# Expert products ordered by part: both chunks' high part first, then both chunks' low part

## The chip, the cores and the metric

The kernel runs on one core of a Trainium2 chip. The metric is the device time in microseconds (us) of one execution.

## The reference, cut to what matters

Two transformer blocks are computed for 256 tokens of width 1024, in float32. The first block ends with a mixture of 32 experts, of which each token takes 4:

```python
def expert_block(args):
    rows, e = args
    xb = xt[rows]
    hb = xb @ w1[e] + b1[e]                       # w1[e]: 1024 x 2048
    g, u = hb[:, :D_EXPERT], hb[:, D_EXPERT:]
    g = jnp.minimum(g, SWIGLU_LIMIT)
    u = jnp.clip(u, -SWIGLU_LIMIT, SWIGLU_LIMIT)
    glu = g * jax.nn.sigmoid(g * SWIGLU_ALPHA)
    return ((u + 1.0) * glu) @ w2[e] + b2[e]      # w2[e]: 1024 x 1024
```

The change touches the products with `w1[e]` and `w2[e]` alone. Ahead of them lie modulation, attention branches and the router; behind them a second block with four SwiGLU feed-forward layers, one more for the context, a neighbourhood attention and a short convolution.

## The kernel before

**Parts.** Float32 accuracy comes from splitting each operand in two numbers of a rounded type (`fp32r`), a high and a low part. For an expert's weight, ScalarE copies the loaded slot into a high buffer (`high`, L895), VectorE subtracts that from the slot and writes the low part over it (`low`, L2258), and TensorE multiplies both with the tokens. The tokens' own two parts lie side by side in the 128 columns of one stationary operand (64 tokens, high and low), and the weights stream past it as the moving operand, 512 columns at a time. So one chunk of 128 rows of weights needs four matmuls: two parts by two halves of 512 columns.

**Slots.** Weights come in slots of 1 MB: two chunks of 128 rows by 1024 columns. They land in a ring of 8 places (`RING2`). There are 4 buffers for high parts (`HIGHS`). A slot's life is: the DMA, issued by SyncE as soon as the slot 8 before it has been used (L679); ScalarE's high part, as soon as the slot 4 before it has been used and the DMA has landed; VectorE's low part; TensorE's 8 matmuls (L1557), the last of which signals "used".

**Turns.** A loop of 16 turns takes two experts each, 0 and 1 of the pair, in 24 slots: 0 to 3 gate of expert 0, 4 to 7 its up projection, 8 to 11 and 12 to 15 the same of expert 1, 16 to 19 the down projection of expert 0, 20 to 23 that of expert 1. Behind the loop stands one more, shorter turn of 12 slots for the busiest expert's further tokens, with the output biases (L1609). A branch for still fuller experts stands behind that, written with the same functions.

**The order on each engine** is written out by hand; each engine works through its own list in order and waits on semaphores.

- TensorE, in `experts`: gate0, up0, gate0 turned; gate1, up0 turned; up1, gate1 turned; first half of down0 (slots 16, 17), up1 turned, second half (18, 19); `gather_next(0)` (L1530, first half of the next pair's tokens, which needs VectorE's selection, L2236 and L2241), `result(0)` (L1594, adds the expert's rows to their tokens, needs ScalarE's copy of the down product); down1 (20 to 23); `gather_next(1)`, `result(1)`. Then the next turn. "Turned" (`turn_rows`, L1572, L1576) are small matmuls that transpose a product.
- ScalarE: high parts, and between them copies of products out of PSUM (`rows`, L920), of the turned selection (L925) and of the gathers (`gathered`, L913), and the Silu (L931). Towards the end of a turn: high 21, 22, rows of down0, gather 0, high 23, high of the next turn's 0, 1, 2, rows of down1, gather 1, high of the next turn's 3. Then the next turn's 4, 5, 6, ahead of which stands a table load in the loop.
- VectorE: low parts 4 to 10, gate of expert 0 (bias L2285, clamp L2291), low 11 to 15, its up half (L2285 to L2300), low 16 to 18, gate of expert 1, low 19, selection, up half, low 20 to 23, low of the next turn's 0 to 3, then the addition of the pair's result (L2309).

The change is in `rows_gemm`, which issues the matmuls of a product, and in what it waits for: `expert_split` counts VectorE's low parts, `expert_high_ready` ScalarE's high parts.

Of the kernel before, what the change touches and what calls it, by code (L numbers as in the profile page):

```python
# [19 lines left out]
DC = D // P  # L20
# [91 lines left out]
TURN_UNITS, TURN_SLOTS, TURN_SIGNALS = len(MOE_UNITS), len(MOE_SLOTS), 18  # L112
# [288 lines left out]
def build(nc, ins, out):  # L401
    with ExitStack() as ctx:
# [5 lines left out]
        def sem(name):  # L408
            if name not in sems:
                sems[name] = ctx.enter_context(nc.semaphore(name))  # L410
            return sems[name]
# [130 lines left out]
        def unit(u):  # L542
            return psum[:, u % 4, :]
# [27 lines left out]
        def slot_ap(s, rows=2, cols=D):  # L571
            return ring[:, PLAN.place[s], 0:rows * cols].rearrange("p (k n) -> p k n", k=rows)

        def high_ap(m, cols):
            return w_high[:, m % HIGHS, 0:2 * cols].rearrange("p (k n) -> p k n", k=2)

        def low_ap(s, cols):
            return w_low[:, PLAN.place[s], 0:2 * cols].rearrange("p (k n) -> p k n", k=2)
# [559 lines left out]
        def _(pe):  # L1138
# [179 lines left out]
            for b in range(TB):  # L1318
                u = U["vnat"] + b
                open_unit(pe, u)  # L1320
                for n, z in enumerate(Z_V + [Z_GATE]):
                    mm = pe.transpose(unit(u)[:, n * P:(n + 1) * P], zT[:, z, b * P:(b + 1) * P], ident)
# [16 lines left out]
            u = U["cmp_hidden"]  # L1339
            open_unit(pe, u)  # L1340
            for m in range(2):
                for j in range(16):
                    if j % 8 == 0:
                        await_slot(pe, PLAN.slots["cmp_w1"] + 2 * m + j // 8)
                    w = slot_ap(PLAN.slots["cmp_w1"] + 2 * m + j // 8, 8, 256)
                    mm = pe.matmul(unit(u)[0:31, 512 * m:512 * m + 2 * P], blocks[:, m, j * 32:j * 32 + 31],
                                   w[:, j % 8, :], start=(j == 0), stop=(j == 15))
# [5 lines left out]
            u = U["cmp_hturn"]  # L1353
            open_unit(pe, u)
            for m in range(2):
                for f in range(2):
                    at = (2 * m + f) * 32
                    mm = pe.transpose(unit(u)[:, at:at + 31], hidden_rows[0:31, m, f * P:(f + 1) * P], ident[0:31, 0:31])
# [3 lines left out]
            u = U["cmp_kv"]  # L1362
            open_unit(pe, u)
            for f in range(2):
                pe.matmul(unit(u)[:, 0:2 * NCMP], w2[:, 0, f, :], hidden[:, 0, f, 0:2 * NCMP],
                          start=(f == 0), stop=(f == 1))
            for g in range(2):
                for f in range(2):
                    mm = pe.matmul(unit(u)[0:NCMP, 512 + g * HD:512 + (g + 1) * HD],
                                   hidden[:, 1, f, g * NCMP:(g + 1) * NCMP], w2[:, 1, f, 0:HD],  # L1370
                                   start=(f == 0), stop=(f == 1))
# [16 lines left out]
            u = U["cmp_scores"]  # L1388
            open_unit(pe, u)
            for b in range(TB):  # L1390
                for g in range(2):
                    rows = slice(64 * g, 64 * g + 64)
                    for j in range(4):
                        at = 512 * g + (b * 4 + j) * 16
                        mm = pe.matmul(unit(u)[:, at:at + NCMP], zT[rows, Z_QC + j, b * P:(b + 1) * P],
                                       kcT[rows, g * NCMP:(g + 1) * NCMP], start=True, stop=True)
# [3 lines left out]
            for b in range(TB):  # L1400
                u = U["cmp_turn"] + b
                open_unit(pe, u)
                for h in range(8):
                    mm = pe.transpose(unit(u)[0:NCMP, h * P:(h + 1) * P], cmpP[:, b * 8 + h, 0:NCMP], ident)
# [82 lines left out]
            for k in range(DC):  # L1487
                if k % 2 == 0:
                    pe.wait_ge(sem("h1_parts"), k // 2 + 1)
                for b in range(TB):  # L1490
                    mm = pe.transpose(unit(U["h_turn"] + b)[:, k * P:(k + 1) * P], hT[:, k, b * P:(b + 1) * P], ident)
                    if k == DC - 1:
                        mm.then_inc(psum_full, 1)
            u = U["logits"]
            open_unit(pe, u)
            for b in range(TB):
                for k in range(DC):
                    mm = pe.matmul(unit(u)[:, b * N_EXPERTS:(b + 1) * N_EXPERTS], hT[:, k, b * P:(b + 1) * P],
                                   rw[:, k, :], start=(k == 0), stop=(k == DC - 1))
# [3 lines left out]
            u = U["positions"]  # L1503
# [10 lines left out]
            u = U["gate_turn"]  # L1514
            open_unit(pe, u)
            for b in range(TB):
                mm = pe.matmul(unit(u)[0:E, b * P:(b + 1) * P], gate2[:, b, 0:E], ident, start=True, stop=True)
# [27 lines left out]
            def experts(c, last=False, over=False):  # L1545
                def rows_gemm(name, j0, x_parts, ks):

                    u = c.unit(name)
                    for k in ks:
                        j = j0 + k // 2  # L1550
                        if k % 2 == 0:
                            pe.wait_ge(sem("expert_split" + c.x), c.turn * TURN_SLOTS + (j + 1))
                        wh, wl = high_ap(j, D), low_ap(PLAN.moe_slot + j, D)
                        for w in (wh, wl):
                            for half in range(2):
                                cols = slice(512 * half, 512 * half + 512)
                                mm = pe.matmul(u[:, cols], x_parts(k), w[:, k % 2, cols], start=(k == 0 and w is wh),  # L1557
                                               stop=(k == DC - 1 and w is wl), skip_group_check=True)
                        if k % 2 == 1:
                            mm.then_inc(c.used if k != DC - 1 else c.full, 1)  # L1560

                def project(name, e, j0):
                    c.open_unit(pe, name)
                    rows_gemm(name, j0, lambda k: xg[:, k, e, :], range(DC))
# [15 lines left out]
                def down(e, ks, j0):  # L1580
                    if ks[0] == 0:
                        pe.wait_ge(sem("expert_hidden" + c.x), c.turn * 2 + (e + 1))
                        c.open_unit(pe, f"down{e}")
                    rows_gemm(f"down{e}", j0, lambda k: hid[e][:, k, :, :].rearrange("p d s -> p (d s)"), ks)
# [129 lines left out]
            for n in range(2):  # L1714
                u = U["na_vturn"] + n
                open_unit(pe, u)
                for b in range(2):
                    for c in range(4):
                        at = (2 * n + b) * P
                        mm = pe.transpose(unit(u)[:, b * 512 + c * P:b * 512 + (c + 1) * P], z2v[:, c, at:at + P],  # L1720
                                          ident)
# [5 lines left out]
            u = U["pool_map"]  # L1727
            open_unit(pe, u)
            for b in range(TB):
                for g in range(4):  # L1730
                    mm = pe.matmul(unit(u)[:, b * 512 + g * P:b * 512 + (g + 1) * P], z2u[:, g, b * P:(b + 1) * P],  # L1731
                                   pw[:, g, :], start=True, stop=True)
# [13 lines left out]
            for s in range(len(NA_STEPS)):  # L1746
                blk, pair = NA_STEPS[s]
                u = U[f"na_turn{s}"]
                await_freed(pe, U[f"na_scores{s}"])
                open_unit(pe, u)  # L1750
                for j in range(2):
                    for kb in range(4):
                        mm = pe.transpose(unit(u)[:, (4 * j + kb) * P:(4 * j + kb + 1) * P],  # L1753
                                          na_probs[s % 2][:, j, kb * P:(kb + 1) * P], ident)
# [4 lines left out]
                u = U[f"na_out{s}"]  # L1759
                open_unit(pe, u)  # L1760
                for j in range(2):
                    h = 2 * pair + j
                    for kb in range(4):
                        mm = pe.matmul(unit(u)[:, j * HD:(j + 1) * HD], na_probsT[:, (4 * j + kb) * P:(4 * j + kb + 1) * P],  # L1764
                                       vnat2[:, kb, h * HD:(h + 1) * HD], start=(kb == 0), stop=(kb == 3))
# [901 lines left out]
```

## Time and profile before

| | |
|---|---|
| median of 3 runs | 2877.54 us (2877.29 to 2879.4) |
| the profiled execution | 2887.47 us, its span 2885.7 us |
| TensorE matmuls busy | 2766.9 us, 96% |
| TensorE weight loads busy | 2479.4 us, 86% |
| VectorE busy | 2107.2 us, 73% |
| ScalarE busy | 1534.3 us, 53% |
| mean granted TensorE clock | 0.969 of full speed |
| moved by DMA | 776.07 MB, 269 GB/s on the mean |

Busy times are those of one profiled execution. The span runs from its first to its last instruction. Matmuls are pipelined and their ends modelled: each matmul of 512 columns has some 396 ns of busy time, although the next one starts much sooner, so TensorE's busy share is not a share of its peak. The shares are means over stages with different limits; the stage of the change runs from 454.8 to 1569.4 us.

### The profile page before, as it was taken

The page shows a single profiled execution, that of the slowest core. Times are in us where ns is not written, and L with a number is a line of the kernel's source. Part 1 is how long each engine was busy: PE and PEld are TensorE (multiplying, and loading weights), DVE is VectorE, ACT ScalarE, POOL GpSimd, SP SyncE. Part 2 cuts the span into 40 slices and gives each one's busy share as a digit, 9 for nine tenths or more (in the row PEclk, how much of TensorE's full clock was granted, in tenths as well). Part 3 has the DMA queues.
Part 4 walks back from the last instruction along what each step waited for, and adds up shares of the span by engine and source line. Part 5 has one row for each costly group of instructions (what it writes and reads, how often), then busy time and mean ns, then how long its engine had stood idle before and what let it go on. Part 6 is the DMA issues. An engine that isn't in the chain of part 4 may idle for free. (4 is left out here: it accounts for less than half of the span.)

```text
span 2885.7 us, 43391 instructions
## 1 busy us (share of the span) xinstructions
PE 2766.9 (96%) x17490; PEld 2479.4 (86%) x17490; DVE 2107.2 (73%) x1863; ACT 1534.3 (53%) x1294; POOL 0.4 (0%) x6
## 2 busy tenths in 40 slices
PE   5999998999999999999999999999999999999998
PEld 4888887877777777777777999999979999999998
DVE  5424648999999999999998877776436756754453
ACT  0023317888888888888885444343434434432442
POOL 0000000000000000000000000000000000000000
PEclk8999998999999999999999999999999999999999
DMA  9743338999999999999996686776416767745451
GB/s 374 255 164 133 116 123 336 376 361 368 381 363 373 379 379 378 379 379 376 374 379 260 223 289 240 269 263 244 166 45 221 277 231 249 284 169 175 149 191 70
DMA packets 172400, 776.07 MB, mean 269 GB/s; under 512 B 12112, under 2 KB 37712, under 8 KB 121328
## 3 DMA queue, kind: packets, MB, share of 16 engines
q1 hardware_dynamic: 168352, 767.08, 70.4%
q10 hardware_dynamic: 3920, 7.11, 0.8%
q8 instruction: 101, 1.65, 0.2%
q14 instruction: 27, 0.22, 0.0%
HBM read 773.10 MB, written 1.05 MB: 268 GB/s over the span
## 5 line engine op out<-in xcount | busy, mean ns | idle before, releaser
L2258 DVE TENSOR_TENSOR w_low<-ring,w_high 128x2048 fp32r<-128x2048 f32 x396 | 882.0, 2286 | 35.5 <-ACT w_high L895 30.7
L895 ACT ACTIVATE w_high<-ring 128x2048 fp32r<-128x2048 f32 x396 | 736.7, 1906 | 89.5 <-PE psum L1557 87.5
L2398 DVE TENSOR_TENSOR w_low<-ring,w_high 128x2048 fp32r<-128x2048 f32 (+1 forms) x199 | 432.6, 2184 | 325.1 <-ACT w_high L1009 322.5
L1009 ACT ACTIVATE w_high<-ring 128x2048 fp32r<-128x2048 f32 (+1 forms) x199 | 362.3, 1829 | 566.1 <-PE psum L1193 486.4
L1193 PE MATMUL psum<-h_high,w_high 128*128 128x256 f32 x2080 | 591.2, 285 | 21.4 <-ACT h_high L1022 21.2
L1193 PE MATMUL psum<-h_high,w_low 128*128 128x256 f32 x2080 | 593.6, 286 | 0.0
L1193 PE MATMUL psum<-h_low,w_high 128*128 128x256 f32 x2080 | 592.6, 287 | 0.0
L1193 PEld LDWEIGHTS psum<-h_high,w_high 128*128 128x128 f32 x2080 | 402.9, 194 | 23.7 <-issue 23.1
L1193 PEld LDWEIGHTS psum<-h_low,w_high 128*128 128x128 f32 x2080 | 397.9, 192 | 0.0
L1193 PEld LDWEIGHTS psum<-h_high,w_low 128*128 128x128 f32 x2080 | 396.6, 191 | 0.0
L1557 PE MATMUL psum<-w_high,xg 128*128 128x512 f32 x1056 | 347.1, 410 | 11.1 <-DVE w_low L2258 3.2
L1557 PE MATMUL psum<-w_low,xg 128*128 128x512 f32 x1056 | 332.2, 396 | 0.0
L1557 PEld LDWEIGHTS psum<-w_high,xg 128*128 128x128 f32 x1056 | 189.4, 188 | 85.0 <-DVE w_low L2258 44.4
L1844 DVE SCALAR_TENSOR_TENSOR mod_sums<-ring,cs,mod_sums 128x1024 f32<-128x1024 f32 x203 | 257.4, 1282 | 5.0 <-DMA ring<-in_mod_w 0.4
L1193 PE MATMUL psum<-m_high,w_high 128*128 128x256 f32 x880 | 248.4, 282 | 0.8 <-DVE arena L2438 0.8
L1193 PE MATMUL psum<-m_low,w_high 128*128 128x256 f32 x880 | 248.0, 282 | 0.0
L1193 PE MATMUL psum<-m_high,w_low 128*128 128x256 f32 x880 | 247.9, 282 | 0.0
L1557 PEld LDWEIGHTS psum<-w_low,xg 128*128 128x128 f32 x1056 | 198.7, 188 | 48.3
L1557 PE MATMUL psum<-w_high,hid 128*128 128x512 f32 x528 | 180.5, 424 | 22.7 <-DVE w_low L2258 20.0
L1557 PE MATMUL psum<-w_low,hid 128*128 128x512 f32 x528 | 169.9, 403 | 0.0
L1193 PEld LDWEIGHTS psum<-m_high,w_high 128*128 128x128 f32 x880 | 166.6, 189 | 1.0 <-DVE arena L2438 0.9
L1193 PEld LDWEIGHTS psum<-m_high,w_low 128*128 128x128 f32 x880 | 166.6, 189 | 0.0
(278 smaller groups left out, 3299.6 us busy)
## 6 DMA issues: line engine op xcount, KB each, us to landing
ring<-in_exp_w SPq DMA_DIRECT2D x396, 1024.0 KB, 7.8
ring<-in_ffn_w SPq DMA_DIRECT2D x135, 1024.0 KB, 5.3
ring<-in_mod_w SPq DMA_DIRECT2D x96, 1024.0 KB, 5.5
ring<-in_ffn_w SPq DMA_DIRECT2D x40, 768.0 KB, 4.8
ring<-in_w_in SPq DMA_DIRECT2D x24, 1024.0 KB, 8.7
ring<-in_even_w_in SPq DMA_DIRECT2D x12, 1024.0 KB, 7.1
ring<-in_conv_w_in SPq DMA_DIRECT2D x12, 1024.0 KB, 5.0
ring<-in_w_branch SPq DMA_DIRECT2D x6, 1024.0 KB, 4.9
```

Of the source, the lines that this page charges most:

```text
L895: act.activation(high_ap(j, D), slot_ap(PLAN.moe_slot + j), ACT.Copy).then_inc(sem("expert_high_ready" + c.x), 1)
L1009: act.activation(high_ap(m, cols), slot_ap(s, 2, cols), ACT.Copy).then_inc(sem("w_high_ready"), 1)
L1193: return pe.matmul(unit(u0 + j // 4)[:, (j % 4) * T:(j % 4 + 1) * T], w[:, k % 2, j * P:(j + 1) * P], h[:, k, :], start=first, stop=stop, ...
L1557: mm = pe.matmul(u[:, cols], x_parts(k), w[:, k % 2, cols], start=(k == 0 and w is wh), stop=(k == DC - 1 and w is wl), skip_group_check=True)
L1844: last = dve.scalar_tensor_tensor(part, w[:, k % 2, :], cond, part, ALU.mult, ALU.add)
L2258: dve.tensor_tensor(low_ap(PLAN.moe_slot + j, D), slot_ap(PLAN.moe_slot + j), high_ap(j, D).bitcast(F32), ALU.subtract).then_inc(sem("expe ...
L2398: dve.tensor_tensor(low_ap(s, cols), slot_ap(s, 2, cols), high_ap(m, cols).bitcast(F32), ALU.subtract).then_inc(sem("w_split"), 1)
```

## The change

The loop over single chunks becomes one over slots. In a slot, all four matmuls with the high part come first, behind a wait for ScalarE's high part of this slot, then all four with the low part, behind the wait for VectorE's low part that stood ahead of the whole slot before. The signal that the slot is used stays on the last of the 8. The starts and stops of accumulation in PSUM follow the first and the last matmul of a half as before.

```diff
-                    for k in ks:
-                        j = j0 + k // 2
-                        if k % 2 == 0:
-                            pe.wait_ge(sem("expert_split" + c.x), c.turn * TURN_SLOTS + (j + 1))
+                    for k0 in ks[::2]:
+                        j = j0 + k0 // 2
                         wh, wl = high_ap(j, D), low_ap(PLAN.moe_slot + j, D)
-                        for w in (wh, wl):
-                            for half in range(2):
-                                cols = slice(512 * half, 512 * half + 512)
-                                mm = pe.matmul(u[:, cols], x_parts(k), w[:, k % 2, cols], start=(k == 0 and w is wh),
-                                               stop=(k == DC - 1 and w is wl), skip_group_check=True)
-                        if k % 2 == 1:
-                            mm.then_inc(c.used if k != DC - 1 else c.full, 1)
+                        for w, ready in ((wh, "expert_high_ready"), (wl, "expert_split")):
+                            pe.wait_ge(sem(ready + c.x), c.turn * TURN_SLOTS + (j + 1))
+                            for k in (k0, k0 + 1):
+                                for half in range(2):
+                                    cols = slice(512 * half, 512 * half + 512)
+                                    mm = pe.matmul(u[:, cols], x_parts(k), w[:, k % 2, cols],
+                                                   start=(k == 0 and w is wh),
+                                                   stop=(k == DC - 1 and w is wl), skip_group_check=True)
+                        mm.then_inc(c.used if k0 != DC - 2 else c.full, 1)
```

## Rows read from the trace of the kernel before

**Rows 1.** One turn: us busy PE, PEld, DVE, ACT, POOL; clock, DMA share, GB/s.

```profile
861.97:929.07 67.10, 65.08 (x326) 52.42 (x325) 64.67 (x47) 56.02 (x38) 0.00 (x0) 1.00 0.94 375
```

**Rows 2.** Waits from 454 to 1577 us: total, times, longest.

```profile
PEld psum L1557 <- DVE w_low L2258: 88.8, 147, 1.5
...
DVE w_low L2258 <- ACT w_high L895: 30.7, 48, 4.8
```

**Rows 3.** Timeline of VectorE: start, duration (of several merged), instructions, idle before.

```profile
859.76 2.29 DVE L2258 TENSOR_TENSOR w_low<-ring,w_high 128x2048 fp32r<-128x2048 f32 x1 [0.21 <-ACT w_high L895]
861.97 2.56 DVE L2309 TENSOR_TENSOR arena<-psum,arena 128x1024 f32<-128x1024 f32 x2
865.57 15.50 DVE L2258 TENSOR_TENSOR w_low<-ring,w_high 128x2048 fp32r<-128x2048 f32 x7 [1.04 <-ACT w_high L895]
...
884.64 8.90 DVE L2258 TENSOR_TENSOR w_low<-ring,w_high 128x2048 fp32r<-128x2048 f32 x4 [0.31 <-ACT w_high L895]
...
907.15 0.90 DVE L2241 TENSOR_TENSOR arena<-sel,small 128x128 f32<-128x128 f32 x4
...
911.14 11.10 DVE L2258 TENSOR_TENSOR w_low<-ring,w_high 128x2048 fp32r<-128x2048 f32 x5
...
1537.40 15.50 DVE L2258 TENSOR_TENSOR w_low<-ring,w_high 128x2048 fp32r<-128x2048 f32 x7 [0.86 <-DVE arena L2309]
```

**Rows 4.** Timeline of TensorE's matmuls, same columns; x2 is a pair.

```profile
853.00 0.73 PE L1557 MATMUL psum<-w_high,hid 128*128 128x512 f32 x2
853.57 0.63 PE L1557 MATMUL psum<-w_low,hid 128*128 128x512 f32 x2
...
854.97 0.34 PE L1530 MATMUL psum<-sel,h_nat_high 128*128 128x128 f32 x2
...
856.70 3.67 PE L1594 MATMUL psum<-arena 128*128 128x256 f32 x16
860.02 0.81 PE L1557 MATMUL psum<-w_high,xg 128*128 128x512 f32 x2
...
898.99 0.73 PE L1557 MATMUL psum<-w_high,hid 128*128 128x512 f32 x2 [1.25 <-DVE w_low L2258]
...
913.72 0.81 PE L1557 MATMUL psum<-w_high,hid 128*128 128x512 f32 x2
```

**Rows 5.** Timeline of ScalarE, same columns.

```profile
857.82 1.90 ACT L895 ACTIVATE w_high<-ring 128x2048 fp32r<-128x2048 f32 x1
862.33 1.28 ACT L895 ACT_TABLE_LOAD   x1 [2.60 <-PE psum L1557]
863.62 5.52 ACT L895 ACTIVATE w_high<-ring 128x2048 fp32r<-128x2048 f32 x3
...
869.95 7.31 ACT L895 ACTIVATE w_high<-ring 128x2048 fp32r<-128x2048 f32 x4
...
908.86 1.03 ACT L920 ACTIVATE arena<-psum 128x1024 f32<-128x1024 f32 x1
...
911.52 1.90 ACT L895 ACTIVATE w_high<-ring 128x2048 fp32r<-128x2048 f32 x1
```

**Rows 6.** Line L1557 from 454 to 1577 us: durations min/median/max, then its idle time.

```profile
L1557 PEld LDWEIGHTS psum<-w_high,xg x1056: 186/187/333, 454.8 to 1547.4; 128*128 128x128 f32 x176
L1557 PE MATMUL psum<-w_high,xg x1056: 389/396/788, 454.8 to 1547.6; 128*128 128x512 f32 x176
...
  DVE w_low L2258: 112.1, 179
```

**Rows 7.** Busy times at and after a turn's boundary, columns as in rows 1.

```profile
858.00:864.00 6.00, 6.00 (x28) 5.00 (x28) 5.67 (x4) 3.39 (x3) 0.00 (x0) 1.00 0.67 208
864.00:912.00 48.00, 46.15 (x237) 37.08 (x236) 45.92 (x38) 43.43 (x31) 0.00 (x0) 1.00 1.00 412
```

**Rows 8.** DMA issues of the page: times, size, median us to landing.

```profile
ring<-in_exp_w SPq DMA_DIRECT2D x396, 1024.0 KB, 7.8
```

**Rows 9.** Timeline of TensorE in another turn, before slot 16.

```profile
1301.62 1.22 PE L1557 MATMUL psum<-w_high,hid 128*128 128x512 f32 x2 [1.26 <-DVE w_low L2258]
```

## The prediction

> **What bounds the kernel now.** I first asked which stretch the edit can touch. The expert products are one line, L1557, and they run from 454.8 to 1569.4 us: 16 turns of 24 weight slots and one of 12. So I read that stretch by turns. Successive additions of an expert pair's result (L2309) lie 67.10 us apart, and in such a turn VectorE is busy 64.67 of 67.10 us, TensorE's matmuls 65.08 (a modelled, overlapping figure), ScalarE 56.02, DMA at 0.94 [rows 1]. Three columns look full, so busy shares do not decide. The list of waits does [rows 2]: TensorE waits for VectorE's low parts (88.8 us at its weight loads), no engine in it waits for a DMA, and VectorE itself waits only 30.7 us in all, always for ScalarE's high part. The scarce engine is VectorE; only its own idle time can be won.
>
> The timeline of VectorE shows where that idle time is [rows 3]. In each turn: 0.21 us before the low part of the next turn's slot 3 (at 859.76), 1.04 us before its slot 4 (at 865.57), 0.31 us before slot 12 (at 884.64). That is 1.56 of the 2.43 us in which it is not busy. Of the stage's 30.7 us, 4.8 are one wait ahead of the first turn's slot 4; the other 25.9 are this pattern 16 times over (25.0, the first of the three being longer in a few turns).
>
> What ends the first two waits? Follow them back. VectorE's low parts of slots 20 to 24 start every 2.21 us from 911.14, so slot 23's begins at 917.78 and ends at 920.07; one turn earlier that is 852.97. TensorE starts slot 23 at 853.00, at once, and hands over to the gather at 854.97; the gather ends at 856.70 and the 16 matmuls of the result at 860.02; there slot 0 of the next turn begins, with no gap since 853.00 [rows 4]. ScalarE meanwhile waits: its copy of the gather (L913) follows the gather, and slot 3's high part follows that copy, at 857.82 to 859.72; and its slot 4 needs the buffer of slot 0, which TensorE gives back at about 862.1; at 862.33, 2.60 us of waiting end with a table load of 1.28, and slot 4's high part ends at about 865.5 [rows 5]. So both waits of VectorE at the boundary hang on one chain: low part of slot 23, TensorE from slot 23 to slot 0, ScalarE, VectorE.
>
> The third wait (0.31) is of another kind: slot 12's high part stands behind ScalarE's Silu, which stands behind VectorE's own clamp (L2291). TensorE is not in it.
>
> **The change, part by part.** Per slot there were 8 matmuls, high and low alternating by chunk, behind one wait for VectorE. Now 4 of them (both chunks' high part) wait for ScalarE only, and 4 for VectorE. The matmul count, their shapes and the place of the release (behind the last) stay.
>
> Removed from the chain: after VectorE has finished slot 23, TensorE used to have the whole slot before it, 853.00 to 854.97. The pairs of matmuls follow 0.467 us apart (853.57 to 854.97 is three) [rows 4], so the four high matmuls are two pairs, 0.93 us. If they are done before the low part arrives, the slot ends 0.93 us earlier, and so does all that follows on the chain, since the gather, the result, slot 0, the table load and the high part follow without slack.
>
> Are they done before? ScalarE is: its high part of slot 23 runs from 911.52 to 913.42 [rows 5], before even slot 20's products begin. TensorE must have time: slot 20 starts at 913.72 [rows 4], and four slots without a gap take 0.65 + 15 x 0.467 = 7.66 us, to 921.38, against 922.07 (854.97 + 67.10) now. On its backlog alone TensorE would win 0.69. But it starts slot 20 earlier too: slots 16 and 17 now wait for their low parts (1.25 us at 898.99), so slot 17, the rows behind it and slots 18 and 19 end 0.93 earlier, at 907.73 in place of 908.66. There the gather must wait for VectorE's selection, which ends at 908.05 [rows 3], and the result behind it for ScalarE's rows, 908.86 to 909.9 [rows 5]; so the result, which takes 3.32 (856.70 to 860.02), starts at about 910.05 in place of 910.40, and slot 20 at 913.37. Without a gap slot 23 would then end at 921.03. The low part allows 920.10 + 0.10 (the longer first step after an open wait: 0.57 against 0.467) + 0.93 = 921.13. The later of the two rules: 922.07 - 921.13 = 0.94 us per boundary. I take 0.93.
>
> What is late next? VectorE's waits at the boundary were 0.21 + 1.04 = 1.25; 0.93 of it goes, the 0.21 wholly and 0.72 of the 1.04, and 0.32 stays before slot 4. The clamp's 0.31 stays. Expected turn: 66.17 us.
>
> Added: a second wait per slot on TensorE, 396 more. What is queued behind it is TensorE's own next products, nothing of another unit overtakes, and a wait that is already met shows no cost now (slots 0 to 3 follow without a step in the timeline). An open one costs up to 0.10. From slot 20 to 23 up to three more may be open; then the backlog end is 921.03 + 0.3 = 921.33 and the gain 0.74. That, or the 0.69 of the backlog without an earlier slot 20, is the lower bound per boundary; the upper bound is all 1.25 us of VectorE's waits there.
>
> Loads of the stationary operand: every matmul has its own, 1056 beside 1056, of 187 ns, and they hide behind the matmuls [rows 6], so the order changes no count. The new order comes back to each activation chunk a second time. The Trainium skill, "TensorE: Matmul & The Clock Gate", section "Part 2: What happens when you issue a matmul", says that a loaded stationary operand can serve many matmuls; by that rule there would be one load for four matmuls now and one for two then. The trace contradicts it here. Taken at its word, with the trace's durations and unhidden, it would be 0.37 us more per slot; the backlog would end at 921.03 + 4 x 0.37 = 922.5, 0.44 later than now, in 15 boundaries 6.6 us: 2884, with a chance of 0.01.
>
> DMA: a slot's place comes back earlier by what the slot ends earlier. From 864 to 912 the DMA engines are full (share 1.00, 412 GB/s), but at the boundary, from 858 to 864, they stand at 0.67 [rows 7]. The change cuts its time out of the boundary, and 24 MB (25.17 million bytes) at 412 GB/s need 61.1 us of a turn of 66.17. Landing takes a median of 7.8 us [rows 8]. The ring of 8 gives slot 10, the tightest I found, 9.6 us: from the release by slot 2, worked out as 860.02 + 0.65 + 11 x 0.467 = 865.8, to ScalarE's reading, the fourth from 869.95, at 875.4 [rows 5]. Both ends move together, so I take nothing.
>
> Sum: 15 boundaries between full turns x 0.93 = 13.95. At the sixteenth, before the turn of 12, VectorE waits 0.21 and then 0.86 for its own register load behind L2309 [rows 3], so only 0.21 is won there. Start: slot 0 of the first turn has both parts ready; nothing. End: down product, biases and result of the last turn start from VectorE's bias addition and have all their weights; nothing. Everything behind the stage starts earlier by the same amount and is not otherwise touched. Gain 14.2 us. Against the profiled execution: 2887.5 - 14.2 = 2873.3, its span 2885.7 - 14.2 = 2871.5 (1.8 us lie around the span). The median of the runs is 9.9 us below the profiled one, none of it in this argument, so for the timed runs: 2877.5 - 14.2 = 2863.3.
>
> **Rivals.** *TensorE's backlog rules* (slot 20 does not start earlier, or open waits cost): 0.69 to 0.74 per boundary, 15 x 0.7 + 0.2 = 10.7, 2866.8. For it: slack over the forecast's chain is only 0.10 us. Against: slots 16 and 17 do wait for VectorE now.
>
> *VectorE is freed wholly*: the high matmuls and fewer restarts save more, all 1.25: 18.9 us, 2858.6. Against it: the table load and high part behind slot 0 cannot shrink.
>
> *The time doesn't move* (within 0.2%, 5.8 us, about what a measurement of this kernel can tell from no change): a gain below 0.37 per boundary. It needs something that takes over at once: the ring's DMA, whose 7.8 us of landing are not far from 9.6, or waits that break the stream of weight loads. For: DMA is full for 48 us of each turn. Against: no wait for a DMA stands in the list. I put it at 2875 to 2878.
>
> *Slower, by the clock.* In each turn TensorE waits 1.25 us before slot 16, and in three turns the granted clock fell there: the pair at 1301.62 takes 1.22 us where the usual one takes 0.73 [rows 4, 9]; that is 1.2 in place of 2.4 GHz. The change turns one pause per slot into two positions, with high matmuls between. If that keeps the clock down longer, TensorE becomes the bound: its pauses for low parts sum to 112.1 us [rows 6], 6.8 per turn, and each microsecond at half clock costs half of one. Beyond 13.6 us at half clock per turn it would be slower than now. At a quarter of the stage, 16.8 us per turn, TensorE needs 60.3 + 8.4 = 68.7 us, 1.6 above now, in 16 turns 25 us: about 2903. By the same page's section "A second HAM failure mode: psum-queue depth-cycling", frequent small pauses between groups of matmuls make the clock swing; the trace now has a dozen pauses a turn and only about 3 us at half clock in three of 16 turns, so it bears that out weakly.
>
> **How the numbers follow.** Forecast 0.60; backlog 0.20; wholly freed 0.04; unmoved 0.11; slower by the clock 0.04, by the loads 0.01. The likeliest is 2863.3. Both bounds of the chain give 2858.6 to 2866.8; half-clock stretches come and go, 0.5 us each in VectorE's pace, 2 us in all. The range runs from 2858 up to 2874, taking in part of the unmoved case. Faster 0.84, same 0.11, slower 0.05.
>
> **What would show it.** Turns of 66.2 us (66.4 in the backlog case) between the L2309 rows; the 0.21 gone and the 1.04 down to 0.3; the 0.31 unmoved; TensorE's slot 23 ending about 1.03 us after VectorE's low part in place of 2.0; ScalarE's wait before the table load 0.9 us shorter in VectorE's time. Wrong it would be if waits for a DMA appear on ScalarE, if gaps appear between matmuls whose waits are met, or if the granted clock in the turns falls below 0.97.

## The result, and the profile after

The median of five runs fell from 2877.64 us (2877.29 to 2881.28) to 2863.85 us (2858.53 to 2866.11). The ratio is 0.9946 with a 95% interval of 0.9932 to 0.9961: 13.8 us, where 14.2 were forecast. The interval holds every gain from 11.2 to 19.6 us, so the times alone do not show the forecast to be right to half a microsecond; the length of a turn does that better. One of the eight runs of `down1_only` below took 4876.45 us at a mean granted clock of 0.75: it counts in that kernel's median of 2871.18 us (2871.00 without it) and not in its ratio.

The same stretch of the changed kernel. First a turn from L2309 to the next, with the columns of [rows 1]:

```profile
922.33:988.50 66.17, 64.47 (x326) 52.58 (x325) 64.60 (x48) 55.66 (x39) 0.00 (x0) 1.00 0.94 380
```

A turn takes 66.17 us in place of 67.10, with the same work on VectorE (64.60 us busy against 64.67): what went is its idle time. The waits of the stage (total, times, longest):

```profile
PEld psum L1557 <- DVE w_low L2258: 63.6, 99, 1.6
...
DVE w_low L2258 <- ACT w_high L895: 15.9, 32, 4.8
```

VectorE waits 15.9 us in place of 30.7, 32 times in place of 48: one of the three waits per turn is gone [rows 2]. The timeline of VectorE shows which (start, duration, instructions, idle before):

```profile
878.21 8.90 DVE L2258 TENSOR_TENSOR w_low<-ring,w_high 128x2048 fp32r<-128x2048 f32 x4 [0.30 <-ACT w_high L895]
...
904.71 17.71 DVE L2258 TENSOR_TENSOR w_low<-ring,w_high 128x2048 fp32r<-128x2048 f32 x8
922.33 2.56 DVE L2309 TENSOR_TENSOR arena<-psum,arena 128x1024 f32<-128x1024 f32 x2
925.30 2.29 DVE L2258 TENSOR_TENSOR w_low<-ring,w_high 128x2048 fp32r<-128x2048 f32 x1 [0.41 <-ACT w_high L895]
```

The eight low parts ahead of L2309 now run in one piece: the wait of 0.21 us among them is the one that is gone. The wait before slot 4 fell from 1.04 to 0.41, the one before slot 12 stands at 0.30 [rows 3]. TensorE, same turn (x4 is half a slot: the four matmuls with the high part or the four with the low part):

```profile
892.55 1.20 PE L1557 MATMUL psum<-w_low,hid 128*128 128x512 f32 x4 [1.15 <-DVE w_low L2258]
...
901.66 0.44 PE L1530 MATMUL psum<-sel,h_nat_high 128*128 128x128 f32 x2 [0.21 <-DVE arena L2241]
...
906.82 1.28 PE L1557 MATMUL psum<-w_high,hid 128*128 128x512 f32 x4
...
912.61 1.10 PE L1557 MATMUL psum<-w_high,hid 128*128 128x512 f32 x4
913.66 1.20 PE L1557 MATMUL psum<-w_low,hid 128*128 128x512 f32 x4
914.70 0.34 PE L1530 MATMUL psum<-sel,h_nat_high 128*128 128x128 f32 x2
...
919.75 1.27 PE L1557 MATMUL psum<-w_high,xg 128*128 128x512 f32 x4
```

Measure each start from the first of the eight low parts, 904.71 here and 911.14 in [rows 3]. Slot 23's low part is written at 904.71 + 3 x 2.21 + 2.29 = 913.63, its four low matmuls start at 913.66, and the gather at 914.70, 9.99 behind the first low part. Before it was 922.07 - 911.14 = 10.93. The slot ends 0.94 us earlier. And ScalarE:

```profile
922.06 1.28 ACT L895 ACT_TABLE_LOAD   x1 [2.60 <-PE psum L1557]
923.35 5.52 ACT L895 ACTIVATE w_high<-ring 128x2048 fp32r<-128x2048 f32 x3
```

The two profiled spans differ by 22.3 us (2885.7 and 2863.4), more than the medians. The stage's last L2309 stands 16.15 us earlier (1533.97 and 1517.82). That is 15 turns at 0.93, three turns of the kernel before that were 0.5 us longer, and 0.64 up to the first L2309 (525.94 and 525.30). The three longer turns, and 0.5 of the 0.64, come from stretches of TensorE at half clock behind slot 16 (from about 696, 1300, 1368 and 496 us); the changed kernel's profile has none there. So some 2 us of the 16.15 are the clock's and not the chain's, and how much of this lies in the medians is not known. The other 6.1 us lie behind the stage, where the code is the same; the profiled execution of before was 9.9 us above its median.

### The profile page after: what moved, and what is told of

It is laid out like the page before. It is cut to its first block, busy times and chain, and to the rows that moved or that the text cites. A ratio compares the mean times of both kernels' runs of the same rounds, so it can differ in the third digit from the quotient of the medians.

```text
span 2863.4 us, 43391 instructions
## 1 busy us (share of the span) xinstructions
PE 2746.3 (96%) x17490; PEld 2469.4 (86%) x17490; DVE 2105.3 (74%) x1863; ACT 1528.8 (53%) x1294; POOL 0.4 (0%) x6
## 4 chain that ended last, share of the span: by engine, by line
PE 67%; DVE 14%; issue 11%; ACT 6%; DMA 1%; DVEq 1%; PEld 0%; ACTq 0%; SPq 0%; PEldq 0%
PE psum L1193 37%; PE psum L1147 7%; DVE w_low L2258 7%; PE psum L1557 6%; PE psum L1333 4%; PE psum L1594 4%; ACT w_high L895 4%; PE psum L1530 2%; PE psum L1272 2%; PE psum L1291 1%; DVE arena L2285 1%; DVE mod_sums L1844 1%; PE psum L1381 1%; PE psum L1428 1%; ACT arena L920 1%
## 5 line engine op out<-in xcount | busy, mean ns | idle before, releaser
L2258 DVE TENSOR_TENSOR w_low<-ring,w_high 128x2048 fp32r<-128x2048 f32 x396 | 880.6, 2285 | 20.7 <-ACT w_high L895 15.9
L1557 PE MATMUL psum<-w_low,xg 128*128 128x512 f32 x1056 | 295.1, 401 | 4.4 <-DVE w_low L2258 3.1
L1557 PE MATMUL psum<-w_high,xg 128*128 128x512 f32 x1056 | 295.3, 401 | 2.7 <-issue 2.7
L1557 PEld LDWEIGHTS psum<-w_low,xg 128*128 128x128 f32 x1056 | 194.3, 188 | 68.0 <-DVE w_low L2258 23.9
L1557 PEld LDWEIGHTS psum<-w_high,xg 128*128 128x128 f32 x1056 | 196.3, 188 | 47.6 <-issue 2.9
L1557 PE MATMUL psum<-w_low,hid 128*128 128x512 f32 x528 | 149.8, 405 | 19.6 <-DVE w_low L2258 18.4
L1193 PEld LDWEIGHTS psum<-m_low,w_high 128*128 128x128 f32 x880 | 166.5, 189 | 0.1
```

The costliest lines, as they stand in the source:

```text
L1193: return pe.matmul(unit(u0 + j // 4)[:, (j % 4) * T:(j % 4 + 1) * T], w[:, k % 2, j * P:(j + 1) * P], h[:, k, :], start=first, stop=stop, ...
L2258: dve.tensor_tensor(low_ap(PLAN.moe_slot + j, D), slot_ap(PLAN.moe_slot + j), high_ap(j, D).bitcast(F32), ALU.subtract).then_inc(sem("expe ...
```

## The experiments

Ratios are to the kernel before, run beside them. A turn is the distance of successive additions of a result, read from the timeline of VectorE; each profile gives 15 of them. The addition is L2309; line numbers shift by a few in some kernels.

**The order without the earlier start.** Both waits of the change replaced by the old one:

```diff
-for w, ready in ((wh, "expert_high_ready"), (wl, "expert_split")):
-    pe.wait_ge(sem(ready + c.x), c.turn * TURN_SLOTS + (j + 1))
+pe.wait_ge(sem("expert_split" + c.x), c.turn * TURN_SLOTS + (j + 1))
+for w in (wh, wl):
```

> The new order of the 8 matmuls (both chunks' high part, then both chunks' low part), but with the old wait: the whole slot waits for VectorE's low part. Theory CHAIN (the gain is VectorE's idle time at the turn's boundary, won because the four high matmuls of slot 23 are done before its low part arrives): nothing is won; turns of 67.10 us, VectorE's wait before slot 4 back at 1.04 us, time as before, 2877.6 us. Rival ORDER (the order itself makes TensorE's work cheaper or steadier): turns near 66.2 us, about 2864 us. Rival by the loads (a stationary operand that returns costs a load): slower than before, some 2884 us.

Measured: 2879.17 us, ratio 1.0008 (0.9995 to 1.0021). Turns of 67.10 us, three of 15 longer (67.56 to 67.62), the wait before slot 4 at 1.04. The order alone does nothing that shows, neither good nor, by returning to each stationary operand, bad.

**One pair ahead.** The old alternation, but its first pair goes behind ScalarE's signal and the other three behind VectorE's:

```diff
+parts = [(k, w) for k in (k0, k0 + 1) for w in (wh, wl)]
+for n, (k, w) in enumerate(parts):
+    if n < 2:
+        pe.wait_ge(sem(("expert_high_ready", "expert_split")[n] + c.x), ...)
```

> The old alternating order, but only the first pair of matmuls (chunk 0, high part) goes ahead of the wait for VectorE, behind a wait for ScalarE. CHAIN: slot 23 ends 0.10 + 3 x 0.467 = 1.50 us after its low part is ready, in place of 1.97, so 0.47 us are won at each of 15 boundaries: turns of 66.63 us, time 2877.6 - 7.2 = 2870.4 us. Rival START (what helps is that TensorE starts on a slot early at all, how much of it is ahead doesn't matter): turns of 66.2 us and 2864 us.

Measured: 2872.45 us, ratio 0.9982 (0.9966 to 0.9997); the interval holds the forecast's 0.9975. The turn is sharper than the time: 66.63 us, as expected (13 of 15 within 0.02; two at 66.80 and 66.99). VectorE's wait before slot 4 is 0.88. Each pair taken ahead of the low part is worth its own 0.467 us.

**The change in the down projections alone**, and **in the gate and up projections alone**. `early` chooses by name between the new order with its two waits and the old order with its one:

```diff
+early = name in ("down0", "down1")        # down_only
+early = name not in ("down0", "down1")    # project_only
```

> The change only in the two down projections (slots 16 to 23 of a turn, 8 of 24); the gate and up projections as before. CHAIN: only slots 16, 17 and 20 to 23 stand on the path to the boundary, so the whole gain stays: turns of 66.17 us, 2863.5 us. Rival EVERYWHERE (each slot that ends earlier gives its place in the ring and its high buffer back earlier, and the gain is the sum over slots): a third of it, turns of 66.8 us, 2873 us.

> The change only in the gate and up projections (slots 0 to 15, 16 of 24); the down projections as before. CHAIN: slot 23 begins only after its low part again, so nothing is won: turns of 67.10 us, 2877.6 us. Rival EVERYWHERE: two thirds of the gain, turns of 66.5 us, 2868 us.

Measured, down projections: 2863.61 us, ratio 0.9957 (0.9941 to 0.9972), all 15 turns within 0.04 of 66.17 us. A third of the slots carries the whole gain. Gate and up projections: 2883.24 us, ratio 1.0027 (1.0014 to 1.0040). Not a gain of two thirds, and not nothing either, as I had expected: slower by some 5 us. Its turns are 67.1 us four times and 67.4 to 67.6 us eleven times. TensorE before slot 16, in a usual turn and in a longer one:

```profile
897.39 0.74 PE L1564 MATMUL psum<-w_high,hid 128*128 128x512 f32 x2 [2.19 <-DVE w_low L2265]
...
1234.26 1.22 PE L1564 MATMUL psum<-w_high,hid 128*128 128x512 f32 x2 [2.17 <-DVE w_low L2265]
1235.28 1.05 PE L1564 MATMUL psum<-w_low,hid 128*128 128x512 f32 x2
```

The projections end 0.94 us earlier, so the pause before slot 16 grew from 1.25 to 2.19 us. From 1234 to 1237 us the granted clock is 0.50 (1.2 in place of 2.4 GHz); at the same place of the turn before, 1167 to 1170, it is 1.00:

```profile
1234.00:1237.00 3.00, 2.74 (x7) 2.17 (x8) 3.00 (x3) 0.58 (x2) 0.00 (x0) 0.50 1.02 423
1167.00:1170.00 3.00, 2.75 (x11) 1.96 (x12) 3.00 (x3) 1.15 (x3) 0.00 (x0) 1.00 1.01 421
```

Read in slices of 2 us, the clock falls behind slot 16's pause in 12 of the 16 turns: in the first turn, and in each of the eleven longer ones.

**The pause filled.** To test that reading, `project_only` with the eight small matmuls of `gate1_turn` done twice, with the same result:

```diff
-for k in range(DC):
+for k in list(range(DC)) * (2 if name == "gate1_turn" else 1):
```

> The kernel of project_only, whose TensorE pauses 2.19 us before slot 16 (1.25 in the kernel before) and most of whose turns last 67.6 in place of 67.1 us; here the 8 small matmuls of gate1_turn are done twice, so that 1.7 us of the pause are filled with work whose result is the same. CLOCK (the longer pause lets the granted clock fall to 1.2 GHz more often, each time 0.5 us for VectorE): nearly all turns back at 67.10 us, 2883.2 - 5 = about 2878 us. Rival: the longer turns come from the ring or from ScalarE, whom the earlier products meet at another time; turns stay at 67.6 us, 2883 us.

Measured: 2878.60 us, ratio 1.0002 (0.9988 to 1.0015), all 15 turns at 67.08 to 67.10 us. The pause is 0.4 us now, and the pair behind it is at full speed in all 16 turns:

```profile
893.67 0.73 PE L1564 MATMUL psum<-w_high,hid 128*128 128x512 f32 x2 [0.39 <-DVE w_low L2265]
```

The clock falls behind slot 16 in none of them, where it fell in 12 turns of `project_only`. More work on TensorE brought the turns back: the loss was the clock's.

**The second down projection alone** (`early = name == "down1"`), run a second time for a profile of the stage.

> The change only in the second down projection (slots 20 to 23). CHAIN with the backlog term: slots 16 and 17 wait for their low parts as before, so slot 20 starts no earlier, TensorE's work on slots 20 to 23 runs without a gap and ends 7.66 us behind its start, 0.69 us earlier than before: turns of 66.41 us, VectorE's wait before slot 4 at 0.65, 2877.6 - 10.6 = 2867.0 us. Rival SLOT23 (only slot 23's own split matters, slots 16 and 17 do nothing): turns of 66.17 us as in the full change, 2863.7 us.

> The kernel of down1_only once more, for a profile of the stage. CHAIN with the backlog term: turns of 66.41 us. SLOT23: 66.17 us. The runs so far (6.4 us gained in place of 10.6) would fit turns of 66.41 us of which some are 0.5 us longer, as in the kernel before, since without the earlier slots 16 and 17 a stretch at half clock on slot 16 still reaches VectorE.

Measured: 2871.18 us, ratio 0.9978 (0.9967 to 0.9989); the second time one run of 2866.77 us, with the profile. Ten of its turns are 66.39 to 66.42 us, as the backlog term says, and five are 0.4 to 1.2 us longer. The clock fell behind slot 16 in three of these five (from about 956, 1354 and 1424 us); the other two follow directly on one of them, so that a fall costs 0.8 to 1.6 us here, over one or two turns, where it cost 0.5 in the kernel before. Slots 20 to 23 run without a gap:

```profile
904.55 1.28 PE L1564 MATMUL psum<-w_high,hid 128*128 128x512 f32 x4
...
912.21 0.34 PE L1530 MATMUL psum<-sel,h_nat_high 128*128 128x128 f32 x2
```

That is 7.66 us, the forecast's figure for four slots without a gap. So SLOT23 falls: slots 16 and 17 are part of the gain, by 0.24 us a turn, and with them changed too no stretch at half clock stands behind slot 16 (none in the changed kernel or in `down_only`). Their share in the medians is larger than I had put it (6.8 us gained, not 10.6). The longer turns explain its direction; their number in other executions is not known, so the size stays open.

**What still keeps VectorE waiting.** Two edits of ScalarE's list on top of the change: a copy of one column as the first thing of a turn, so that the table load comes before the wait for slot 0, and the Silu two high parts later:

```diff
+act.activation(stats[:, 3, 15, 0:1], ones[:, 0:1], ACT.Copy)    # table_early
 high(c, 4, 5, 6)
 ...
-high(c, 11)
+high(c, 11, 12, 13)                                              # silu_later
 swish(0)
-high(c, 12, 13, 14)
+high(c, 14)
```

> The changed kernel, and ScalarE begins each turn with a copy of one column (of constants, into a column of statistics that nothing reads here), so that its table load (1.28 us) falls into its wait for slot 0 in place of behind it. CHAIN: slot 4's high part comes 1.28 us earlier, VectorE's remaining 0.41 us of waiting at the boundary go, turns of 65.76 us, 15 x 0.41 = 6.2 us less than the changed kernel, 2857.7 us. Rival DMA (the ring can't deliver a turn's 25.17 million bytes faster than now): turns stay at 66.17 us and ScalarE gets waits for a DMA; 2863.9 us.

> The changed kernel with ScalarE's Silu of expert 0 behind the high parts of slots 12 and 13 in place of ahead of them. If the remaining 0.30 us before slot 12 hang on the Silu and not on TensorE: they go, turns of 65.87 us, 16 x 0.30 = 4.8 us less than the changed kernel, 2859.0 us. Rival: the Silu comes late for VectorE's up half or for slot 14, and a wait of the same size appears there; 2863.9 us.

> The changed kernel with both edits, the early table load and the later Silu. If VectorE is the bound and its idle time all there is to win: no wait of VectorE is left inside the turns, turns of 65.46 us, 11.0 us less than the changed kernel, 2852.9 us. Rival DMA: turns stop at a length above that (25.17 million bytes at 412 GB/s are 61.1 us, at the 385 GB/s that the changed kernel's best slices show 65.4 us), with waits for a DMA on ScalarE.

Measured, Silu later: 2858.36 us, ratio 0.9930 (0.9915 to 0.9945), turns of 65.78 us. The wait before slot 12 is gone, and 0.39 us with it, 0.09 more than the wait had shown. Early table load: 2862.95 us, ratio 0.9952 (0.9937 to 0.9968); turns stay at 66.17 us, and not for the DMA. ScalarE first, then VectorE:

```profile
910.11 1.28 ACT L945 ACT_TABLE_LOAD   x1
911.41 0.20 ACT L945 ACTIVATE stats<-consts 128x1 f32<-128x1 f32 x1
912.71 5.58 ACT L895 ACTIVATE w_high<-ring 128x2048 fp32r<-128x2048 f32 x3 [1.10 <-PE psum L1558]
```

```profile
912.96 2.57 DVE L2310 TENSOR_TENSOR arena<-psum,arena 128x1024 f32<-128x1024 f32 x2
915.94 15.50 DVE L2259 TENSOR_TENSOR w_low<-ring,w_high 128x2048 fp32r<-128x2048 f32 x7 [0.41 <-DVE arena L2310]
```

Slot 4's high part is ready at about 914.6 and VectorE starts at 915.94, 2.98 us behind its own addition, as without the edit (922.33 to 925.30). Both theories I had written down fall: with ScalarE ready 1.3 us before, the 0.41 is VectorE's own. With both edits: 2855.61 us, ratio 0.9924 (0.9911 to 0.9938), turns of 65.78 us, as with the Silu alone.

**VectorE's loop with two turns in its body**, on top of both edits:

```diff
-with dve.Fori(0, PAIRS) as i:
-    steps.enter(i, 7)
-    experts(first_turn(i), steps)
+with dve.Fori(0, PAIRS // 2) as i:
+    steps.enter(i, 14)
+    experts(first_turn(i * 2), steps)
+    experts(first_turn(i * 2 + 1), steps)
```

> The kernel of both_waits, and VectorE's loop over the 16 turns written as 8 rounds of two turns. In both_waits the 0.41 us ahead of slot 4 stayed although its high part was ready 1.3 us before. LOOP (they are VectorE's jump back and the registers of its next turn): at every second boundary they shrink to 0.1 or less, turns of 65.78 and 65.4 us in alternation, 8 x 0.3 = 2.4 to 2.8 us less than both_waits, 2853 us. Rival OWN WAIT (they are its wait for its own last addition to be written): all turns stay at 65.78 us, 2855.6 us.

Measured: 2854.53 us, ratio 0.9921 (0.9905 to 0.9936), the fastest of all; from `both_waits` the time alone doesn't tell it apart. The turns do: 65.50 and 65.87 us in alternation, where I had expected 65.4 and 65.78. Inside the body, then at the jump:

```profile
1044.60 2.56 DVE L2310 TENSOR_TENSOR arena<-psum,arena 128x1024 f32<-128x1024 f32 x2
1047.31 15.50 DVE L2259 TENSOR_TENSOR w_low<-ring,w_high 128x2048 fp32r<-128x2048 f32 x7
...
1110.10 2.56 DVE L2310 TENSOR_TENSOR arena<-psum,arena 128x1024 f32<-128x1024 f32 x2
1113.17 13.30 DVE L2259 TENSOR_TENSOR w_low<-ring,w_high 128x2048 fp32r<-128x2048 f32 x6 [0.51 <-DVE arena L2310]
```

Inside, slot 4 follows 2.71 us behind the addition, at the jump 3.07 (0.51 idle). So the wait is not for the addition itself, which stands ahead of the same low part inside the body too: the larger part of the 0.41 is the jump and the registers of the next turn. The jump with two turns costs 0.09 more than with one (3.07 against 2.98), so a third of the 0.27 won inside is given back; why it costs more is not shown.

## Why the prediction was right

**The bound** was named rightly: VectorE, whose busy time per turn stayed at 64.5 to 64.7 us in the changed kernel and in all ten experiments, while its idle time went from 2.42 down to 1.57 in the changed kernel and to 1.00 at the least. The turn changed with that idle time, whichever engine the edit was on.

**The chain** low part of slot 23, TensorE to slot 0, ScalarE, VectorE is shown by its parts: nothing is won without slots 16 to 23 (`project_only`), everything with them alone (`down_only`), half with one pair (`one_pair`, 66.63 us), nothing by the order (`order_only`).

**0.93 us per boundary.** Slot 23 ends 0.94 us earlier and turns are 0.93 us shorter. The low matmuls start 0.03 us after the low part and take 1.04; the prediction had 0.03 and 1.03.

**The backlog.** The prediction's figures hold: 7.66 us for four slots without a gap (7.66 in `down1_again`), 0.69 us without an earlier slot 20 (turns of 66.40). With the whole change slot 20 starts 2.11 behind the first low part in place of 2.58, 0.47 earlier; I had 0.35. The gather waits for the selection, 0.21, as foreseen.

**Where a step failed.** "0.93 of it goes, the 0.21 wholly and 0.72 of the 1.04, and 0.32 stays before slot 4", with 1.25 us as the upper bound. The 1.04 fell by 0.63 and 0.41 stayed. The missing 0.09 stands at the first wait: the eight low parts in one piece take 17.62 us to L2309's start, with the wait 17.93, so the shown 0.21 had cost 0.31. And what stays is not only ScalarE's high part, ready at about 923.35 + 1.90 = 925.25, but VectorE's own turn of the loop, which alone gives 925.30 (`table_early`). Two limits met within 0.05 us: the chain's reckoning came out, and it is luck that VectorE's own limit, which the prediction did not have between full turns, lay no higher. With 0.41 not to be won by this change, the case "VectorE is freed wholly" (18.9 us) could not have happened: the most was 0.94 a boundary, which is what came. The number was right with less room above it than I gave, and the measured 13.8 us standing so near 14.2 is in part luck too, given the interval and the half-clock stretches that come and go.

**The sum.** 15 x 0.93 = 13.95 is measured as such, in the turns that no half-clock stretch lengthened. At the sixteenth boundary L2309 and the next low part lie 3.42 us apart, 3.43 before: VectorE's own 0.86 stayed, as said. The 0.21 us forecast beside it came as 0.31: each run of eight low parts ahead of an addition is that much shorter, and there are sixteen of them to fifteen full turns.

**Rivals.** The loads: `order_only` denies them, at 1.0008, and in the changed kernel too each matmul has its own load (1056 beside 1056 for each part on the tokens, 187 to 188 ns). The clock: it did not turn the change, but the mechanism is real in this kernel, `project_only` is the case. Two of the prediction's figures on it were misread. The 112.1 us of pauses, 6.8 a turn, add up waits seen at the weight loads (88.8 us, 147) and at the matmuls (23.3 us, 32), which are the same pauses before slots 12 and 16 seen twice; the loads' 88.8 us, 5.4 a turn, are the ones to take. And the clock had fallen behind slot 16 in four of the 16 turns, not three. The Trainium skill, "TensorE: Matmul & The Clock Gate", section "A second HAM failure mode: psum-queue depth-cycling", lays such swings to many small pauses between groups of matmuls. The traces agree by half. `project_filled` has 129 waits for low parts at its weight loads and no fall behind slot 16, `project_only` has 83 and twelve falls, the kernel before 147 and four. So the falls do not go with the number of pauses but with the long one before slot 16. Its length and the work put into it changed together, so the runs do not tell these two apart. DMA: the median landing of an expert's slot rose from 7.8 to 8.3 us, and no wait for one appears in the changed kernel. With the early table load a few do, 1.5 us in all in `table_early` and 2.8 in `unrolled`, and in `both_waits`, in its first turn:

```profile
ACT w_high L895 <- DMA ring<-in_exp_w: 1.3, 2, 0.8
```

## What to carry to other kernels

The engine that bounds a loop may still be idle for a microsecond at one place of it. Follow that wait back through all engines: the few instructions on this path are the only ones whose order brought a gain (here 8 slots of 24). Before you count a wait as winnable, ask what the waiting engine itself has to do there: the loop's jump hid behind a wait that was put down to another engine. And work that ends earlier without being on the path can cost: it lengthens a pause elsewhere, and TensorE's clock may fall behind it.

## What I had not expected of the hardware

- **TensorE's clock fell behind some pauses of one or two microseconds, and more often behind the longer ones.** Pause before slot 16's first waiting matmul, and in how many of the profile's 16 turns the granted clock fell behind it, towards 0.50: 0.33 and 0.39 us, none (`down_only`, `project_filled`); 0.88 us, none (`silu_later`, `both_waits`, `unrolled`); 1.15 us, none (the changed kernel, `table_early`); 1.25 us, four in the kernel before, three in `order_only`, one in `one_pair`, three in `down1_again`; 2.19 us, twelve (`project_only`). A fall made the turns some 0.3 to 0.5 us longer in most of these kernels, and 0.8 to 1.6 in `down1_again`. These are single profiles, so the counts are rough.
- **The jump of VectorE's loop** leaves 0.41 us idle with one turn in the body, 0.51 with two, against 0.15 where the same two instructions follow inside the body (1044.60 + 2.56 to 1047.31). The last two belong to one profile, `unrolled`.
- **An instruction of VectorE that need not wait starts some 0.08 us before the one ahead has ended** (861.97 against 859.76 + 2.29). A wait costs that overlap as well: 0.31 us for a shown 0.21, 0.39 for a shown 0.30.
